# Hybrid attention/S5/MoE step on one core: a planner with VectorE's queue in its model, S5 units split, and output products that begin with the S5 rows

## The chip, the cores and the metric

The kernel runs on one core of a Trainium2 chip. The metric is device microseconds (us) of one execution. The kernel before took 1464.19 us (median of 3 runs, 1458.98 to 1472.08).

## The reference, cut to what matters

One layer, for a prompt of 1024 tokens (no cache) and for 8 decode sequences with one token each and 8192 cached positions in pages of 128. D = 1024, all data float32.

```python
hn = rmsnorm(x, ln1_g)
proj = hn @ w_in                      # columns: q 512 | k 512 | v 512 | u 512
q, k = rope_partial(q, pos) * 64**-0.5, rope_partial(k, pos)
# differential attention, 4 heads, two score maps a head (c = 0, 1)
s = einsum('bqhcd,bkhcd->bhcqk', q, k);  p = softmax(where(mask, s, -1e30))
a = p[:, :, 0] - lam * p[:, :, 1]
attn = subln(einsum('bhqk,bkhe->bqhe', a, v)) * (1 - lambda_init)
# S5: 32 groups of 16 channels, a 64-dim complex diagonal state each
a_cum, h = associative_scan(combine, (lam_bar, b_bar @ u));  h = h + a_cum * h0
y = gelu(real(c @ h) + d_skip * u);  s5_out = y * sigmoid(y @ w_glu + b_glu)
x = x + concatenate([attn, s5_out], -1) @ w_out      # rows 0:512 attention, 512:1024 S5
# top-1 of 4 groups, top-2 of 8 experts in it, 32 gated-MLP experts
x = x + hier_moe(rmsnorm(x, ln2_g), ...)
y = rmsnorm(x, ln_f_g)                # also returned: new k, v, last S5 states
```

## The kernel before, in words

Everything ahead of the experts is one long stage in which three kinds of work share the engines. The work is cut into *units*; `make_plan` (line 181) puts them in one order, `PLAN`, and TensorE, VectorE and GpSimd each walk through that same order and do their part of each unit; ScalarE walks through `ACT_PLAN`, the same units sorted by a modelled time (lines 262 and 263). Nothing is reordered at run time: an engine that waits for a semaphore in one unit holds back all later units on that engine.

`streams` (line 81) holds the lists, each unit with its TensorE cost and what must have ended how many us before it. `make_plan` is greedy: of the list heads that are ready it takes the one whose list stands first (`dec, C, O, T, S, qt, fin, s5, proj, q, late`), otherwise the one that is ready soonest. Only TensorE's time is kept; the time of the other engines stands in the lags. The lists are:

- `dec`: the decode attention. 64 units `K` (two passes over 4 sequences) and 64 units `V`, each with 8 pages of 256 KB of the cache, which SyncE loads into `ring` (16 slots) with line 500 as TensorE frees them. Between them `m1`, `m2`, `m3`, `pt` (row maximum, exp, transposes), and at the end `ov`, `dout`, `dout2`, `out(8)` (the decode rows' output product), `hT(8)`, `r(8)`. In the plan two K/V units stand at least `PACE` = 7.1 us apart.
- `proj` and `q`: products of the input projection in halves of 4 k-tiles (8 matmul records each), `kt`/`qt` transposes after VectorE's rotation.
- `S`, `C`, `T`, `O` for each of 8 query tiles i and 4 heads h: scores (TensorE), row maximum (VectorE, lines 1139 to 1145), exp (ScalarE, line 828), combination of the two maps (`C`, VectorE, lines 1152 to 1157), transposes (`T`, line 1919), copy (ScalarE, line 837), product with V (`O`); after the fourth head a root on GpSimd (line 563) and `AN` (line 1180), `ot` (line 1937).
- `s5`: `s5a` (tables, VectorE) and four rounds n of `bU` (GpSimd loads U in small pieces, line 618), `bA`, `bP`, `bK` (a product; VectorE adds `dd` at line 1381; GpSimd spreads the result with 8 loads, line 633), `bE`, `bX(n, 0..3)`, `bH` (VectorE: 12 passes over 512 columns with 8 scans between them, and small ones for the last states, lines 1396 to 1428), `bY(n, 0..1)`, `bG`, `bS`; `ld1` brings the result back for `glu`.
- `late`: `ld2` (first half of `w_out`, after the last `q`), `glu`, `ld3` (after the last `O`: second half of `w_out` at line 663, then the 8 tiles of x and the decode rows at lines 668 and 669), then for each of 8 row tiles i `out(i, a, f)`: column half a, k half f, 4 matmuls of 512 columns. A product keeps its PSUM bank from f = 0 to f = 1. `out` on TensorE (line 2099) waits for both halves of `w_out` and for all attention tiles; VectorE's addition to x (line 1463) waits for all x tiles.
- `fin`: `hn`, `hs`, `hT`, `r` for each tile (norm, transposes, router product), then the routing: `pick1`, `pick2`, `rank`, `rt0`, `rt1`, `ids`, `lists`, `turn0`.

`psum_keys` gives each unit its PSUM banks: six banks are handed out in a ring in plan order, and `hold` (line 174) is the planner's guess how long after the unit's end a bank stays taken. In `make_plan` the decode pages have a model of their own:

```python
land.append(max(land[-1], t + PAGE_LAG) + PAGE_US)     # 3.6, 6.0
due = max(due + PACE, t - 2 * PACE)                    # 7.1
```

In SBUF the first half of `w_out` lies where `w_q` was, the second where the attention's probabilities `P` are; x tiles 0 to 3 lie over `kT`, 4 to 7 over `V`. After that stage an expert loop runs over 4 experts at a time (3 MB of weights each), its first product waiting for the router of the decode rows; then the results are gathered and normed.

Of the kernel before, what the change touches and what calls it, by code (L numbers as in the profile page):

```python
# [18 lines left out]
SPP = 4  # L19
# [60 lines left out]

def streams():

    dec = [(("dprep",), 2.5, [(("dq",), 6.0)])]
    for x in range(NPASS):
        for t in range(TURNS):
            for g in range(2):
                for y in range(SPP):
                    dec.append((("K", x, t, g, y), 1.95, [(("ov", SPP * x - 1), 0.8)] if x else [(("dprep",), 0.5)]))
        dec += [(("m1", x), 0.8, [(dec[-1][0], 0.9)]), (("m2", x), 0.3, [(("m1", x), 3.3)]),
                (("m3", x), 0.3, [(("m2", x), 1.0)]), (("pt", x), 2.3, [(("m3", x), 3.2)])]  # L90
        for y in range(SPP):
            b = SPP * x + y
            for t in range(TURNS):
                for g in range(2):
                    late = [(("pt", x), 1.2)] if t + g + y == 0 else [(("ov", b - 2), 1.2)] if t + g == 0 and y >= 2 else []
                    dec.append((("V", x, y, t, g), 1.95, late))
                    if y and t == 0 and g == 1:
                        dec.append((("ov", b - 1), 0.5, [(("V", x, y - 1, TURNS - 1, 1), 2.5)]))
        dec.append((("ov", b), 0.5, [(("V", x, y, TURNS - 1, 1), 2.5)]))
    dec += [(("dout",), 0.1, [(("ov", NB - 1), 1.0)]), (("dout2",), 0.2, [(("dout",), 2.0)]),  # L100
            (("out", NT), 4.0, [(("dout2",), 1.0), (("out", NT - 1, 1, 1), 0.0)]), (("hn", NT), 0.0, [(("out", NT), 2.0)]),
            (("hs", NT), 0.0, [(("hn", NT), 2.5)]), (("hT", NT), 1.0, [(("hs", NT), 0.8)]),
            (("r", NT), 1.1, [(("hT", NT), 0.6), (("r", NT - 1), 0.0)])]
# [22 lines left out]
    qt = [(("qt", i), 0.6, [(("q", i, 1), 3.5)] + ([(("S", i - 1, H - 1), 0)] if i else [])) for i in range(NT)]  # L126
# [3 lines left out]
    for n, (i, h) in enumerate(heads):  # L130
        w = 0.128 * (i + 1)
        x = [(("qt", i), 1.5)] + ([(("O",) + heads[n - 2], 0)] if n >= 2 else [])
        S.append((("S", i, h), 0.28 + 0.22 * (i + 1), x))
        C.append((("C", i, h), 0.0, [(("S", i, h), 3.3 + 3.0 * w)]))
        T.append((("T", i, h), 0.14 * (i + 1), [(("C", i, h), 0.9 + 1.1 * w)]))
        x = [(("T", i, h), 0.5 + 0.8 * w)]
        if h == 0 and i:
            x.append((("ot", i - 1), 0))
        O.append((("O", i, h), 0.2 + 0.37 * (i + 1), x))
        if h == H - 1:  # L140
            O += [(("AN", i), 0.0, [(("O", i, h), 3.0)]), (("ot", i), 0.66, [(("AN", i), 0.8)])]

    s5 = [(("s5a",), 0.0, [(("dprep",), 2.0)])]
    for n in range(NQ):
        x = [(("bY", n - 1, 1), 0)] if n else [(("u", 3, 1, 1), 4.0), (("dk2",), 3.0), (("s5a",), 60.0)]
        s5 += [(("bU", n), 0.0, x + [(("u", n, 1, 1), 3.0)]), (("bA", n), 0.0, x), (("bP", n), 1.1, [(("bA", n), 5.0)]),
               (("bK", n), 2.1, [(("bA", n), 11.0)]), (("bE", n), 0.0, [(("bK", n), 2.5)])]
        s5 += [(("bX", n, j), 0.75, [(("bP", n), 2.2), (("bU", n), 14.0)]) for j in range(JQ)]
        s5 += [(("bH", n), 0.0, [(("bX", n, JQ - 1), 1.2)])]
        s5 += [(("bY", n, 0), 3.5, [(("bH", n), 13.5), (("bK", n), 13.0)]), (("bG", n, 0), 0.0, [(("bY", n, 0), 2.0)]),  # L150
               (("bY", n, 1), 3.5, []), (("bG", n, 1), 0.0, [(("bY", n, 1), 2.0)]),
               (("bS", n), 0.0, [(("bG", n, 1), 1.5)])]
# [2196 lines left out]
```

## Time and profile before

| | us |
|---|---|
| median of 3 runs | 1464.19 (1458.98 to 1472.08) |
| the profiled execution, own time | 1464.86 |
| its span | 1463.1, mean granted clock 0.94 |
| busy: TensorE / weight loads / VectorE / ScalarE / GpSimd | 1279.2 / 670.6 / 521.6 / 248.5 / 214.7 |
| DMA | 458.31 MB, mean 313 GB/s |
| K and V pages | 1024 transfers of 256 KB, 4.7 us each to land |

Times in the profile count from the span's start. A line is that of the helper for most matmuls (line 1800), so matmuls are told apart by tile and by their place in time; one float32 matmul leaves two records, a transpose one. The granted clock is TensorE's, 1.00 being the level of 2.4 GHz and 0.50 that of 1.2 GHz.

### The profile page before, as it was taken

What the parts mean: (1) busy time and instruction counts of PE and PEld (TensorE: products, weight loads), DVE (VectorE), ACT (ScalarE), POOL (GpSimd) and SP (SyncE); (2) the same over time, 40 slices, a digit from 0 to 9 for tenths busy, and PEclk for the clock granted to TensorE, in tenths of its full rate; (3) what the DMA queues carried; (4) which work ended last, traced back from release to release, by engine and by line L of the source; (5) the groups of instructions that cost most, each with busy time, mean ns of one, the idle gap of its engine ahead of it and who ended that gap; (6) DMA issues with size and microseconds to landing.
All of it is one profiled execution on the core that took longest, in us unless ns stands there. A gap on an engine that the chain in (4) does not pass through costs nothing.

```text
span 1463.1 us, 26568 instructions
## 1 busy us (share of the span) xinstructions
PE 1279.2 (87%) x9000; PEld 670.6 (46%) x9000; DVE 521.6 (36%) x1413; ACT 248.5 (17%) x476; POOL 214.7 (15%) x329
## 2 busy tenths in 40 slices
PE   7999999999869799998869999976899999999930
PEld 4545555554324346666544444433444444444410
DVE  2723543253365455553512111153122111121126
ACT  2101111121212233332212000000011111111111
POOL 2003140313100200000010000001122222222211
PEclk9999999999989999998999999976999999999975
DMA  9989998869968999999996998998899999999764
GB/s 364 329 310 293 321 294 283 272 198 298 298 227 304 352 338 363 365 315 323 331 387 228 330 336 293 322 349 321 277 324 371 360 354 363 361 363 366 256 211 179
DMA packets 185201, 458.31 MB, mean 313 GB/s; under 512 B 23953, under 2 KB 24337, under 8 KB 176530
## 3 DMA queue, kind: packets, MB, share of 16 engines
q1 hardware_dynamic: 163602, 390.21, 75.4%
q0 software_dynamic: 21504, 66.78, 13.8%
q8 instruction: 66, 1.08, 0.3%
q14 instruction: 29, 0.24, 0.0%
HBM read 421.92 MB, written 33.80 MB: 311 GB/s over the span
## 4 chain that ended last, share of the span: by engine, by line
PE 70%; DMA 12%; DVE 7%; SPq 5%; issue 3%; DVEq 2%; ACT 1%; POOL 0%; ACTq 0%; POOLq 0%
PE WA L1800 52%; PE SC L1800 7%; PE OD L1800 7%; DMA ring<-in_cacheK 6%; SPq L500 4%; DMA qpad<-h_scratch,idc 3%; DMA ring<-in_cacheV 2%; PE WA L2166 2%; DVE arena L1769 1%; PE WA L1919 1%; DVE arena L1782 1%; DVE st L1141 1%; PE WA L2126 1%; DMA arena<-y_scratch 1%; DVEq L1771 1%
## 5 line engine op out<-in xcount | busy, mean ns | idle before, releaser
L1800 PE MATMUL WA<-arena 128*128 128x512 f32 (+10 forms) x1440 | 353.4, 432 | 17.6 <-issue 7.2
L1800 PE MATMUL WA<-arena,xm 128*128 128x512 f32 (+3 forms) x816 | 313.6, 581 | 8.4 <-DMA arena<-in_w_out 6.5
L1800 PEld LDWEIGHTS WA<-arena 128*128 128x128 f32 (+2 forms) x1440 | 191.6, 195 | 155.0 <-issue 135.5
L1800 PEld LDWEIGHTS WA<-arena,xm 128*128 128x128 f32 (+1 forms) x816 | 124.4, 174 | 162.8 <-issue 154.7
L1800 PE MATMUL WA<-xm,arena 128*128 128x512 f32 x192 | 87.3, 603 | 1.7 <-ACT arena L958 1.3
L1800 PE MATMUL OD<-ring,sall 128*32 128x512 f32 x512 | 71.0, 670 | 15.0 <-DMA ring<-in_cacheV 15.0
L563 POOL TENSOR_TENSOR st<-st,consts 128x1 f32<-128x1 f32 (+2 forms) x18 | 13.8, 765 | 466.2 <-DVEq L1175 280.0
L1800 PE MATMUL OD<-ring,qpad 128*32 128x128 f32 x2048 | 67.9, 285 | 15.7 <-DMA ring<-in_cacheK 15.7
L1800 PEld LDWEIGHTS OD<-ring,qpad 128*32 128x32 f32 x2048 | 56.6, 114 | 35.9 <-DMA ring<-in_cacheK 18.4
L1800 PE MATMUL SC<-ring,qpad 128*32 128x128 f32 x2048 | 64.9, 278 | 9.1 <-DMA ring<-in_cacheK 9.0
L1712 DVE TENSOR_TENSOR xm<-WA,colw 128x960 f32<-128x960 f32 x16 | 18.5, 1158 | 147.2 <-PE WA L2166 147.2
L1712 DVE TENSOR_TENSOR arena<-WA,colw 128x960 f32<-128x960 f32 x16 | 18.5, 1158 | 139.5 <-PE WA L2166 139.3
L1800 PEld LDWEIGHTS SC<-ring,qpad 128*32 128x32 f32 x2048 | 55.0, 111 | 24.5 <-issue 12.0
L1800 PE MATMUL SC<-ring,sall 128*32 128x512 f32 x512 | 61.4, 598 | 2.2 <-DMA ring<-in_cacheV 2.2
L828 ACT ACTIVATE arena<-WA,st 128x128 f32<-128x128 f32 (+7 forms) x64 | 47.4, 740 | 80.0 <-DVEq L1145 77.9
L686 POOL DMA_DIRECT2D y_dec<-arena x32 | 17.8, 556 | 271.7 <-ACT arena L965 271.7
L1800 PE MATMUL WA<-ring,xm 128*128 128x512 f32 x128 | 56.3, 592 | 0.0
L1800 PE MATMUL WA<-xm 128*128 128x512 f32 x128 | 56.3, 592 | 0.0
L965 ACT ACTIVATE arena<-WA 128x1024 f32<-128x1024 f32 x32 | 32.7, 1023 | 128.7 <-PE WA L1800 128.7
L1800 PEld LDWEIGHTS WA<-xm,arena 128*128 128x128 f32 x192 | 35.4, 192 | 41.6 <-issue 40.1
L1463 DVE TENSOR_TENSOR arena<-arena,WA 128x512 f32<-128x512 f32 x16 | 11.0, 688 | 113.9 <-PE WA L1800 113.9
L1141 DVE TENSOR_REDUCE st<-WA 128x1 f32<-128x128 f32 (+7 forms) x64 | 48.5, 758 | 5.1 <-issue 0.4
(364 smaller groups left out, 1244.1 us busy)
## 6 DMA issues: line engine op xcount, KB each, us to landing
ring<-in_cacheK SPq DMA_DIRECT2D x512, 256.0 KB, 4.7
ring<-in_cacheV SPq DMA_DIRECT2D x512, 256.0 KB, 4.7
arena<-in_w_gu SPq DMA_DIRECT2D x16, 2048.0 KB, 9.8
arena<-in_w_dn SPq DMA_DIRECT2D x16, 1024.0 KB, 14.3
ring<-in_w_gu SPq DMA_DIRECT2D x8, 2048.0 KB, 10.3
xm<-in_w_gu SPq DMA_DIRECT2D x8, 2048.0 KB, 10.5
ring<-in_w_dn SPq DMA_DIRECT2D x8, 1024.0 KB, 14.8
xm<-in_w_dn SPq DMA_DIRECT2D x8, 1024.0 KB, 14.8
```

The source lines that it names most:

```text
L500: sp.dma_start(ring[:, GRP * half + j, :], cache[bass.ds(pages[j], 1), :, :] .rearrange("a p n -> p (a n)")).then_inc(s_pg[PARTS * half + ...
L686: gp.dma_start(io["y_dec"][bass.ds(4 * NB * q + NB * v, NB), :], yb[v % 2][CAP:128, :]).then_inc(m_sd[v % 2], 16)
L828: act.activation(P[:, n % 2, c, 0:w], slot("S", i, h, c)[:, 0:w], ACT.Exp, bias=st[:, 4 * (n % 2) + c:4 * (n % 2) + c + 1], scale=HD ** -0 ...
L965: act.activation(yb[v % 2], W[1][:, :], ACT.Copy).then_inc(m_ys, 1)
L1141: dve.reduce_max(st[:, 8 + c:9 + c], S[:, 0:w], AX)
L1712: dve.tensor_tensor(hgT[v % 2][:, :, 0:CAP], (W[0] if src is None else src)[:, :] .rearrange("p (k n) -> p k n", k=KD)[:, :, 0:CAP], colw[ ...
L1769: dve.scalar_tensor_tensor(x1[0:r, i, :], yg[i][c][0:r, :], wts[0:r, c, i:i + 1], x1[0:r, i, :], MUL, ADD)
L1771: dve.drain()
L1782: dve.scalar_tensor_tensor(x1[0:r, i, :], x1[0:r, i, :], st[0:r, i:i + 1], lnf[0:r, :], MUL, MUL)\
L1800: return pe.matmul(out, lhsT, rhs, start=first, stop=last, **kw)
L1919: last = pe.transpose(slot("AT", i, h)[:, 128 * j:128 * j + 128], P[:, n % 2, 0, 128 * j:128 * j + 128], ident)
L2166: last = pe.transpose((W[0] if out is None else out)[:, 128 * k:128 * k + CAP], hg[v % 2][0:CAP, 128 * k:128 * k + 128], ident[0:CAP, 0:CAP])
```

## The change

The planner gets VectorE's time. `vector_us(unit)` gives for each unit the us that VectorE needs and the lag from TensorE's end to its start; `make_plan` keeps `busy`, the end of VectorE's queue in plan order, and records `end[("dve",) + unit]`. Dependencies that stood on lags after TensorE's end now stand on VectorE's end, and banks are counted free from there. TensorE costs of T, O, bY, bX, bK, rank, ids and others are changed too.

```diff
+def vector_us(unit):
+    ...
+    if k in ("u", "k", "q", "out") and (len(a) == 1 or a[-1] == 1):
+        return {"u": (1.1, 0.2), "k": (1.25, 0.95), "q": (1.25, 0.95), "out": (0.75, 0.2)}[k]
+    return {
+        "S": (1.95 + 0.265 * i, 0.2), "C": (0.95 + 0.133 * i, 0.0), "O": (1.35 if a[1:] == (H - 1,) else 1.15, 0.2),
+        "AN": (0.7, 0.0), "s5a": ((4.0, 9.0, 9.0, 9.0)[i if k == "s5a" else 0], 3.0 if a == (1,) else 0.0),
+        "bA": ((4.0, 5.0)[a[1] if k == "bA" else 0], 0.0), "bE": (3.9, 0.0), "bK": (0.3, 1.3),
+        "bH": ((3.7, 3.0, 5.6)[a[1] if k == "bH" else 0], 0.0), "bY": (0.75, 0.9), "bG": (0.75, 0.8),
+        ...
+    }.get(k)
...
-        w = 0.128 * (i + 1)
-        x = [(("qt", i), 1.5)] + ([(("O",) + heads[n - 2], 0)] if n >= 2 else [])
+        w = 0.115 * (i + 1)
+        x = [(("qt", i), 1.0)] + ([(("O",) + heads[n - 2], 0)] if n >= 2 else [])
         S.append((("S", i, h), 0.28 + 0.22 * (i + 1), x))
-        C.append((("C", i, h), 0.0, [(("S", i, h), 3.3 + 3.0 * w)]))
-        T.append((("T", i, h), 0.14 * (i + 1), [(("C", i, h), 0.9 + 1.1 * w)]))
-        x = [(("T", i, h), 0.5 + 0.8 * w)]
+        C.append((("C", i, h), 0.0, [(dve("S", i, h), 0.9 + w)]))
+        T.append((("T", i, h), 0.12 * (i + 1), [(dve("C", i, h), 0.25)]))
+        x = [(("T", i, h), 0.5 + w)]
...
-        O.append((("O", i, h), 0.2 + 0.37 * (i + 1), x))
+        O.append((("O", i, h), 0.2 + 0.21 * (i + 1), x))
...
+    late += [(("ldx",), 0.0, [(("S", NT - 1, H - 1), 0.1)])]
+    o7 = [(("ld3",), 0.0, [(("O", NT - 1, H - 1), 0.1)])]
...
-        x = [(("ld3",), 9.0), (("glu", 4, 0), 2.5), (("ot", NT - 1), 1.0)]
-        late += [(("out", i, a, f), half, x) for a in range(2) for f in range(2)]
+        x = [(("ldx",), 7.0), (("ld2",), 16.0), (dve("glu", 4, 0), 0.2)], [(("ld3",), 8.0), (("ot", i), 1.6)]
+        late += [(("out", i, a, f), half, x[f]) for f in range(2) for a in range(2)]
...
-        end[unit] = t
+        end[unit] = done = t
+        if vector_us(unit):
+            us, lag = vector_us(unit)
+            end[("dve",) + unit] = done = busy = max(busy, t + lag) + us
...
-                free[b] = t + hold(unit)
+                free[b] = done + hold(unit)
```

S5 units are split: `s5a` into four parts (a generator that yields), `bA` into two (before and after `s_pA`), `bH` into three: the products before the scans, the scans, the rest. Their instructions are the same, in the same order among themselves; other units can stand between the parts. GpSimd's stores of `bH` belong to the last part.

```diff
-            def bH(n):
+            def bH(n, p):
...
+                if p == 0:
+                    dve.wait_ge(s_Xs, JQ * (n + 1))
...
+                    return
+                if p == 1:
+                    for j in range(JQ):
...
+                    return
```

The output products take the S5 rows (k tiles 4 to 7) first, and `w_out`'s halves are loaded in that order; each half has a semaphore of its own. x tiles 0 to 3 are loaded after the last `S`, the others with `ld3`. In the plan both column halves do f = 0, then both f = 1.

```diff
             def ld2():
                 gp.wait_ge(*filled("q", NT - 1))
-                gp.dma_start(wout[:, 0:4, :], io["w_out"][:, 0:4, :]).then_inc(s_wo, 16)
+                gp.dma_start(wout[:, 0:4, :], io["w_out"][:, 4:8, :]).then_inc(s_wo, 16)
+
+            def ldx():
+                gp.wait_ge(*filled("S", NT - 1, H - 1, 1))
+                for i in range(4):
+                    gp.dma_start(x1[:, i, :], io["x_p"][i, :, :]).then_inc(s_x1, 16)
 
             def ld3():
                 gp.wait_ge(*filled("O", NT - 1, H - 1))
-                gp.dma_start(wout[:, 4:8, :], io["w_out"][:, 4:8, :]).then_inc(s_wo, 16)
+                gp.dma_start(wout[:, 4:8, :], io["w_out"][:, 0:4, :]).then_inc(s_wo2, 16)
...
-                for i in range(NT):
+                for i in range(4, NT):
...
             def out_(i, a=0, f=0):
                 if f == 0:
-                    pe.wait_ge(s_wo, 32)
-                    pe.wait_ge(s_mix, NT)
+                    pe.wait_ge(s_wo, 16)
                     pe.wait_ge(s_mix2, 9)
+                else:
+                    pe.wait_ge(s_wo2, 16)
+                    pe.wait_ge(s_mix, i + 1)
```

## Rows read from the trace of the kernel before

**Rows 1.** Windows, stages: length, busy PE PEld DVE ACT POOL, PEclk, DMA share, GB/s
```profile
377.00:748.00 371.00, 319.99 (x3322) 186.19 (x3323) 196.79 (x542) 105.29 (x232) 25.44 (x40) 0.94 0.92 324
748.00:951.00 203.00, 193.29 (x998) 85.71 (x997) 32.46 (x60) 14.57 (x28) 11.69 (x22) 0.97 0.88 312
951.00:1025.00 74.00, 51.97 (x334) 26.04 (x327) 34.70 (x114) 2.53 (x5) 5.44 (x7) 0.72 0.92 335
1025.00:1463.00 438.00, 367.49 (x1088) 176.33 (x1085) 104.52 (x225) 64.58 (x115) 87.31 (x105) 0.93 0.88 315
```
**Rows 2.** Timeline of TensorE: the first K unit, the routing's ids product, the last V units
```profile
43.70 3.70 PE L1800 MATMUL SC<-ring,qpad 128*32 128x128 f32 x128
...
993.46 7.07 PE L1800 MATMUL WA<-arena 128*128 128x52 f32 x32 [4.11 <-DVEq L1669]
1000.46 5.11 PE L1800 MATMUL OD<-ring,sall 128*32 128x512 f32 x32
```
**Rows 3.** Waits of TensorE, 30 to 1025 us: total, times, longest
```profile
PE OD L1800 <- DMA ring<-in_cacheK: 15.7, 7, 4.2
PE OD L1800 <- DMA ring<-in_cacheV: 15.0, 8, 5.8
PE WA L1919 <- DVEq L1159: 14.3, 3, 11.1
PE SC L1800 <- DMA ring<-in_cacheK: 9.0, 6, 2.5
PE WA L1937 <- DVEq L1181: 7.6, 4, 3.4
...
PE WA L1800 <- DMA arena<-in_w_out: 6.5, 1, 6.5
```
**Rows 4.** Windows inside the attention stage and at the pass's turn
```profile
390.00:440.00 50.00, 35.70 (x174) 14.21 (x172) 31.34 (x106) 8.75 (x27) 2.49 (x3) 0.83 0.64 226
440.00:750.00 310.00, 274.08 (x3130) 168.23 (x3132) 159.64 (x419) 94.00 (x197) 20.75 (x33) 0.96 0.96 339
780.00:790.00 10.00, 10.00 (x39) 5.36 (x38) 1.17 (x4) 6.15 (x11) 0.00 (x0) 1.00 0.01 3
```
**Rows 5.** Timeline of TensorE, 417 to 436 us: T(1,0) and q(3,0)
```profile
429.05 0.69 PE L1919 MATMUL WA<-consts,arena 128*128 128x128 f32 x2 [11.13 <-DVEq L1159]
429.53 5.55 PE L1800 MATMUL WA<-arena,xm 128*128 128x512 f32 x8
```
**Rows 6.** Timeline of VectorE, 414 to 429 us: first and last of bH(3), then C(1,0)
```profile
414.17 0.69 DVE L1396 TENSOR_TENSOR arena<-arena 128x512 f32<-128x512 f32 x1
...
420.98 0.69 DVE L1410 TENSOR_TENSOR arena<-arena 128x512 f32<-128x512 f32 x1
...
426.10 0.29 DVE L1428 TENSOR_TENSOR rt<-rt,arena 128x32 f32<-128x32 f32 x2
...
428.47 0.49 DVE L1157 SCALAR_TENSOR_TENSOR arena<-arena,st 128x256 f32<-128x256 f32 x1
```
**Rows 7.** Timeline of TensorE: the first output products, and a K unit between them
```profile
756.93 5.77 PE L1800 MATMUL WA<-arena,xm 128*128 128x512 f32 x8 [6.48 <-DMA arena<-in_w_out]
...
766.33 1.08 PE L1800 MATMUL OD<-ring,qpad 128*32 128x128 f32 x32 [2.62 <-DMA ring<-in_cacheK]
767.59 5.37 PE L1800 MATMUL WA<-arena,xm 128*128 128x512 f32 x8 [0.18 <-PE OD L1800]
...
773.99 3.70 PE L1800 MATMUL WA<-arena,xm 128*128 128x512 f32 x8
```
**Rows 8.** GpSimd's last issues before the output products: w_out's second half, x
```profile
746.42 0.59 POOL L663 DMA_DIRECT2D arena<-in_w_out  x1
747.01 4.16 POOL L668 DMA_DIRECT2D arena<-in_x_p  x8
```
**Rows 9.** VectorE's waits before line 1381 (bK of the four S5 rounds)
```profile
  ACT arena L894: 27.4, 2
  DMA arena<-in_ddiag: 17.3, 2
```

More of the change, by code:

```diff
@@ L125, in streams @@
         qs += [(("q", i, 0), half, x), (("q", i, 1), half, [])]
[L126 removed]
+    qt = [(("qt", i), 0.5, [(dve("q", i, 1), 0.3)] + ([(("S", i - 1, H - 1), 0)] if i else [])) for i in range(NT)]
     S, C, T, O = [], [], [], []
@@ L144, in streams @@
+    s5 = [(("s5a", 0), 0.0, [(dve("dprep"), 0.0)])] + [(("s5a", p), 0.0, [(dve("s5a", p - 1), 1.3)]) for p in range(1, 4)]
     for n in range(NQ):
[L145 to L148, printed above, removed]
@@ new lines, in streams @@
+        late += [(("out", i, a, f), half, x[f]) for f in range(2) for a in range(2)]
+        fin += [(("hn", i), 0.0, [(dve("out", i, 1, 1), 0.1)]), (("hs", i), 0.0, [(dve("hn", i), 0.9)]),
+                (("hT", i), 0.95, [(dve("hs", i), 0.25)]), (("r", i), 0.6, [(dve("hT", i), 0.25)])]
+    fin += [(("pick1",), 0.0, [(dve("r", NT - 1), 0.1)]), (("pick2",), 0.0, [(dve("pick1"), 0.0)]),
+            (("rank",), 4.7, [(dve("pick2"), -1.5)]), (("rt0",), 0.0, [(("rank",), 0.3)]), (("rt1",), 0.0, [(dve("rt0"), 0.0)]),
+            (("ids",), 6.9, [(dve("rt1"), 0.3)]), (("lists",), 0.0, [(("ids",), 0.3)]),
+            (("turn0",), 1.0, [(("lists",), 14.0), (("out", NT), 0.0)])]
@@ L171, in streams @@
+    return {"dec": dec, "o7": o7, "C": C, "O": O, "T": T, "S": S, "qt": qt, "fin": fin, "s5": s5, "proj": proj, "q": qs,
             "late": late}
 def hold(unit):
-    k, w = unit[0], 0.128 * (unit[1] + 1) if len(unit) > 1 else 0
-    return {"S": 3.0 + 3.0 * w, "T": 0.5 + 0.8 * w, "O": 0.5, "pt": 1.3, "bY": 5.0, "bP": 1.5, "bK": 1.6,
-            "bX": 0.8, "q": 0.8, "k": 0.8, "v": 0.8, "hT": 1.5, "out": 1.0}.get(k, 1.0)
+    k, w = unit[0], 0.115 * (unit[1] + 1) if len(unit) > 1 else 0
+    return {"S": 0.7 + w, "T": 0.5 + w, "O": -0.5, "pt": 1.3, "bP": 1.5, "bK": 1.0, "out": 0.1, "u": 0.1, "hT": 0.1, "r": 0.1,
+            "bX": 0.8, "q": -0.4, "k": -0.4, "v": 0.9, "ot": 1.4, "glu": -0.8, "ids": 4.0, "rank": 16.0}.get(k, 1.0)
@@ L187, in make_plan @@
     land, gone, due = [4.0, 10.0], [], 4.0
-    kept, never = {}, 1e9
+    kept, never, busy = {}, 1e9, 0.0
     def place(unit):
@@ L226, in make_plan @@
         for b in kept.get(unit, []):
-            free[b] = t + 1.0
+            free[b] = done + hold(unit)
         if unit[0] in "KV":
@@ L259, in hymba_step @@
     SPOT, USES = banks(PLAN)
-    ready = {u: ends.get(u, ends.get(u[:-1], 0.0)) + (2.4 if u[0] == "S" else 0.0) for u in PLAN}
+    ready = {u: ends[("dve",) + u] - (0.9 + 0.13 * u[1]) if u[0] == "S" else ends.get(u, ends.get(u[:-1], 0.0)) for u in PLAN}
     ACT_PLAN = sorted(PLAN, key=lambda u: ready[u])
@@ L1264, in cmul, with s5a_parts @@
                 dve.drain()
-            def s5a():
+            def s5a_parts():
                 dve.wait_ge(s_ld5, 32)
```

145 lines of the change are left out of this document (83 added, 62 removed), and 3 rows, old and new, of the table i.

## The prediction

> **What bounds the kernel now.** I read the busy times of the windows first, to find the stages [rows 1]. The change can act only on what lies ahead of the experts, the first 1025 us; the 438 us behind are an expert loop whose code stays as it is, and I carry them over. Before 1025 us two resources are nearly full. TensorE is busy 320.0 of 371 us in the attention stage (377 to 748 us) and 193.3 of 203 us around the output products (748 to 951 us); the DMA engines have shares of 0.92 and 0.88 there. Neither is the bound alone, so what counts is where each of them stands still.
>
> Next the list of who waited for whom on TensorE [rows 3]. Its largest rows are waits for K and V pages: 15.7 + 15.0 + 9.0 = 39.7 us. Waits on VectorE come second: 14.3 us before T units and 7.6 us before `ot`. Then 6.5 us once for `w_out`. Only the second and third kind are what the change speaks of.
>
> The decode stream is the other end of the stage. Its first K unit starts at 43.7 us and its last V unit ends at 1000.46 + 5.11 = 1005.6 us [rows 2]: 961.9 us for 128 units, 7.5 us each. The planner puts them 7.1 us apart, in both kernels, so 128 x 7.1 = 909 us is the least that this plan allows, and 961.9 - 909 = 53 us is the most that any rearrangement within the pace can bring. So the ceiling is 53 us, before any stall is named.
>
> **The change part by part.** The sum is made against the profiled execution's own 1464.9 us (span 1463.1 us), which is 0.7 us above the median of the runs; that difference is far below what can be measured, and I forecast both alike.
>
> *A. bH in three parts, VectorE in the plan.* TensorE stood 11.1 us before T(1,0), and the q half behind it ran at 1.2 GHz for a part: 5.55 us [rows 5] in place of 3.70 us for the same 8 records [rows 7], 1.85 us more. The reason is in VectorE's timeline [rows 6]: from 414.17 to 426.4 us it works on bH(3) without a gap, and C(1,0), for which T(1,0) waits, is done only at 428.96 us. Split, the attention's units can stand between the parts, whose longest is the third, 420.98 to 426.4 us, 5.4 us. DMA was not full here: share 0.64 in 390 to 440 us [rows 4], so the ring had nowhere to load, and what TensorE gains the stream gains too. Bounds: 0 (the next plan has the same collision elsewhere) to -13.0 us (11.1 + 1.85). I take -11: near the full row, less 2 us for a part that is still in the way.
>
> *B. The small VectorE waits of the attention stage.* T has 14.3 - 11.1 = 3.2 us left, `ot` 7.6 us: 10.8 us [rows 3]. But from 440 to 750 us the DMA share is 0.96 [rows 4], so only 0.04 x 310 = 12 us of the stream's time is free there, and TensorE's K units are met by missing pages anyway. Most of this gain turns into a longer wait for K. Bounds: -10.8 to +6 us (a new order can place as many new waits as half of the old ones); I take -3.
>
> *C. Output products begin with the S5 rows.* Before, the first half product starts at 756.93 us after 6.5 us of waiting for `w_out`, takes 5.77 us, the next 5.37 us, and one at the full clock 3.70 us [rows 7]: 6.5 + 2.1 + 1.7 = 10.2 us lost. Now the S5 rows' half of `w_out` is there (loaded after the last q), and out(0,0,0) and out(0,1,0) can run as soon as the last scores are made, so 2 x 3.6 = 7.2 us of work fill the hole, and the halves behind it come after work rather than after a gap. More than two halves cannot go: in the list the third needs the attention rows, which are issued at 746.42 us [rows 8] as before, since their place is held by P. VectorE's wait for all x tiles goes too, but it had banks to spare and I cost it at nothing; the cover is the 5 other banks. The stage behind is TensorE's (193.3 of 203 us), so what is saved goes through, up to the stream: its share of 0.88 there [rows 1] leaves 0.12 x 203 = 24 us. Bounds: 0 to -14 us (both numbers above, partly overlapping); I take -8.
>
> *D. The tail.* The routing holds TensorE 4.1 us before `ids`, and the last 2 V units stand behind its 7.07 us [rows 2], pages landed or not. The plan's new costs for rank, ids and the routing on VectorE may put V ahead. Bounds: -5 to +4 us, the wait itself in either direction; I take -2.
>
> *E. x tiles 0 to 3 ahead of the last K units.* 2 MB now start with the last scores, some 15 us before the 746.42 us of before, in a stretch whose DMA share is 0.96 [rows 4]. At 339 GB/s of that row they take 6.2 us, which the K units there wait, and which ld3 has less behind. The net is a wait moved from beside the output products into the attention chain. Bounds: 0 to +6 us; I take +3. The Trainium skill (DMA: Bandwidth & Descriptors, Issuing engines are not separate DMA queues) says that transfers issued by GpSimd and by SyncE run on the same 16 engines and interleave; by it an earlier start on GpSimd's queue frees nothing as long as the pages fill the engines. The trace agrees with the direction: a K unit waits 2.62 us while `w_out` and x are in flight [rows 7].
>
> *F. Instructions.* s5a, bA and bH issue what they did; two semaphores and one wait are new, nothing that an engine would show. The S5 loads and their 8 small pieces a round stay, and so does most of the 39.7 us for pages.
>
> Sum: -11 - 3 - 8 - 2 + 3 = -21 us, so 1464.9 - 21 = **1444 us**. All lower ends give -13 - 10.8 - 14 - 5 = -43 us, 1422; all upper ends +6 + 4 + 6 = +16 us, 1481.
>
> **The rivals.**
>
> *Rival 1: the page stream takes it all back, 1460 us.* For it: the pace of 7.1 us is unchanged, 0.96 of DMA in the second half of the attention, and pages are already TensorE's largest wait. Then A's gain is spent waiting for pages by 750 us, C's work fills time in which K is late anyway, and only some 5 us remain, 1464.9 - 5 = 1460. Against it: the share of 0.64 over 50 us, and 0.01 over the 10 us from 780 [rows 4]: there is DMA time to recover.
>
> *Rival 2, the slower side: VectorE stands in S5's loads with the attention behind it, 1480 us.* Before line 1381 (bK) VectorE waited 27.4 + 17.3 = 44.7 us over the four rounds, for GpSimd's U loads and for a product [rows 9]. These were free, since TensorE had projection halves that need nothing of VectorE. The new plan counts VectorE's busy time but nothing of how late a load is in traffic: bK has 1.3 us and 0.3 us in its table. If it packs rounds 2 and 3 against scores and combinations, each such wait holds up the S and C units queued behind it on VectorE, then T and O on TensorE and `out`. It decides the sign from the point where 21 of the 44.7 us, 47%, are exposed; at 80% the price is 36 us, 1444 + 36 = 1480. Against it: three of the four rounds lie before the attention, where no unit of TensorE hangs on VectorE closely. The Trainium skill (Perfetto Trace Analysis, Tensor Engine Instruction (MATMUL, LD_WEIGHTS)) says that VectorE's execution FIFO is strict, unlike TensorE's; by this more places to stand in, now nine parts where there were three units, speak against the split. Rows 6 show such a queue: C(1,0) came behind all of bH(3).
>
> *Rival 3: VectorE's and `w_out`'s waits all go and the stream follows, 1427 us.* 11.1 + 1.85 + 10.8 + 10.2 + 4.1 = 38 us, 1464.9 - 38 = 1427, within the ceiling of 53. It needs a greedy order that is right nearly everywhere, and pages that come earlier in a stretch with 0.96.
>
> **How the numbers follow.** About 1% (14.6 us) is what a measurement of this kernel can tell from no change; the bound for faster is 1449.6 us. The forecast's case, 1432 to 1455 us, has 0.55, of which 0.44 lies below 1449.6. Rival 1 has 0.22, rival 2 0.13, rival 3 0.10. Faster: 0.44 + 0.10 = 0.54; within 1%: 0.11 + 0.22 = 0.33; slower: 0.13. The predicted time is the likeliest case's, 1444. The range for 8 in 10 takes in that case, rival 1 and a part of either outer case, 1425 to 1470: below, 1422 and 1427 bound it; above, half of rival 2's price, 1444 + 18 = 1462, and some of the +16 us sum.
>
> **What would show it.** Right: no wait over 4 us of a T unit on line 1159, and DMA share over 0.8 in the 50 us around the fourth bH; two output halves before the last `ot`, and both f = 1 halves at 3.7 us; the last V ends near 985 us instead of 1005.6 and the experts start near 1004. For rival 1: waits for pages above 50 us in the same list and a last V later than 997 us. For rival 2: VectorE's wait before line 1381 or 1396 ending in the attention stage, with T or `ot` waiting just then. For E: K waits over 3 us between 725 and 745 us beside x loads. I would be wrong altogether if the new plan moves S5's fourth round so late that `glu`, and with it the S5 rows, is not ready when the scores end.

## The result: 1% slower, and the profile after

| | before | after |
|---|---|---|
| median of the runs | 1463.0 us | 1479.1 us (1478.3 to 1481.8) |
| ratio after to before | | 1.0118 [1.0077, 1.0158] |
| span of the profiled execution | 1463.1 us | 1477.4 us |
| the 128th V unit, V(1,3,3,1), ends | 1005.6 us | 1018.9 us |
| last router product r(8) ends | 1025.5 us | 1040.0 us |

The forecast was 1444 us with a range of 1425 to 1470; the change costs 16 us and lies outside. The ratios, here and below, leave out runs in a slower state that now and then befalls any kernel, and they differ from the ratios of the medians by up to 0.3%. Behind r(8) the two traces have 437.6 and 437.4 us, so all of the 14.3 us between the spans comes from the part ahead of the experts.

The same stages as [rows 1], after the change, then the 50 us of the fourth bH [rows 4] and two stretches at the turn of the pass (columns as in [rows 1]):

```profile
377.00:748.00 371.00, 341.15 (x3257) 198.03 (x3256) 189.36 (x532) 105.01 (x229) 21.93 (x34) 0.94 0.91 320
748.00:951.00 203.00, 190.71 (x1063) 88.45 (x1061) 38.46 (x76) 15.76 (x30) 13.30 (x23) 0.98 0.84 292
951.00:1025.00 74.00, 52.90 (x240) 19.00 (x240) 25.56 (x91) 0.24 (x1) 1.39 (x2) 0.59 0.95 348
390.00:440.00 50.00, 47.24 (x253) 21.33 (x246) 22.22 (x80) 9.35 (x26) 11.18 (x21) 1.00 0.97 344
725.00:775.00 50.00, 38.81 (x483) 25.27 (x483) 12.32 (x28) 8.20 (x16) 6.37 (x11) 0.90 1.02 379
775.00:805.00 30.00, 28.35 (x148) 14.96 (x150) 8.28 (x18) 7.34 (x13) 1.63 (x3) 1.00 0.25 92
```

The hole at 390 to 440 us is closed: TensorE busy 47.2 us in place of 35.7, DMA share 0.97 in place of 0.64. And in 775 to 805 us the DMA engines stand: share 0.25. TensorE's waits, 30 to 1025 us, as [rows 3]:

```profile
PE OD L1861 <- DMA ring<-in_cacheK: 20.0, 9, 4.1
PE OD L1861 <- DMA ring<-in_cacheV: 15.0, 13, 5.0
PE WA L1980 <- DVEq L1199: 13.9, 7, 3.4
PE SC L1861 <- DMA ring<-in_cacheV: 13.9, 8, 3.8
PE SC L1861 <- DMA ring<-in_cacheK: 4.2, 3, 2.2
PE WA L1861 <- DVEq L1730: 2.8, 1, 2.8
PE WA L1861 <- DMA arena<-in_w_out: 2.5, 1, 2.5
```

The single wait of 11.1 us before a T unit (now line 1980) is gone, its longest is 3.4 us, but there are seven that add up to 13.9 us where three made 14.3. Pages: 53.1 us where [rows 3] with its smaller rows has 41.9.

**Where the 14 us arise.** I laid each unit of the planner's order onto TensorE's records. Three lengths add up to the end: the end of the last K unit, the turn of the pass from there to the end of V(1,0,0,0), and the V phase from there to r(8).

| us | last K unit | turn | V phase | r(8) |
|---|---|---|---|---|
| before | 767.4 | 25.1 | 233.0 | 1025.5 |
| after | 773.3 | 31.4 | 235.3 | 1040.0 |

So 5.9 us in front of the last K unit, 6.3 us in the turn, 2.3 us behind. Meanwhile the last output product ends 10.8 us earlier (940.0 for 950.8) and `ids` 7.3 us earlier, for nothing: TensorE then waits for V pages, 5.0 us once and 0.8 us before each of the last five groups.

**The turn.** TensorE's timeline after the change. pt(1) is line 2048; in it ScalarE's exponentials of the whole pass are transposed, so nothing of V(1) can start before it:

```profile
777.27 1.18 PE L1861 MATMUL OD<-knT,qpad 128*32 128x8 f32 x32
778.38 3.70 PE L1861 MATMUL WA<-arena,xm 128*128 128x512 f32 x8
782.03 3.60 PE L1861 MATMUL WA<-arena,xm 128*128 128x512 f32 x8
785.56 0.38 PE L1861 MATMUL OD<-consts,rt 1*128 1x1 f32 x2
785.87 3.70 PE L1861 MATMUL WA<-arena,xm 128*128 128x512 f32 x8
789.40 1.04 PE L2190 MATMUL WA<-consts,arena 128*128 128x128 f32 x8
790.28 3.60 PE L1861 MATMUL WA<-arena,xm 128*128 128x512 f32 x8
793.71 1.87 PE L1861 MATMUL WA<-wr,arena 128*128 128x36 f32 x16
795.41 3.68 PE L1861 MATMUL WA<-arena,xm 128*128 128x512 f32 x8
798.93 0.60 PE L2048 MATMUL WA<-consts,sall 128*128 128x128 f32 x4
```

ScalarE's side, where the exponentials end at 788.5 us and the copies of pt (line 905) follow 11 us later:

```profile
786.20 2.00 ACT L896 ACTIVATE sall<-sall,mrow 128x2048 f32<-128x2048 f32 x1 [6.75 <-DVEq L1248]
788.20 0.28 ACT L898 ACTIVATE snew<-snew,mrow 128x8 f32<-128x8 f32 x1
799.57 2.69 ACT L905 ACTIVATE sall<-WA 128x512 f32<-128x512 f32 x4 [10.99 <-PE WA L2048]
```

Between 788.5 and 798.9 us TensorE runs the end of an output half, hT(0), a half, r(0) and another half. It isn't waiting; the planner put them there, because pt takes five of the six PSUM banks at once. The change makes a tile's f = 0 halves first, for both column halves, and then the f = 1 halves, so two banks are held by unfinished sums at a time and a third is just being opened: in its plan pt(1) stands behind out(1,1,1), r(0) and out(2,0,0). pt(1) comes only 10.4 us after its input. In the kernel before, out(1,0,0) had just ended and pt(1) began at 785.0 us, 0.4 us behind the exponentials. During the extra time the ring is full and no page is loaded, which is the share of 0.25.

### The profile page after: what moved, and what is told of

Its sections match the earlier page's. It is cut to its first block, busy times and chain, and to the rows that moved or that the text cites. A ratio compares the mean times of both kernels' runs of the same rounds, so it can differ in the third digit from the quotient of the medians.

```text
span 1477.4 us, 26567 instructions
## 1 busy us (share of the span) xinstructions
PE 1301.8 (88%) x9000; PEld 681.8 (46%) x9000; DVE 521.8 (35%) x1413; ACT 248.3 (17%) x476; POOL 214.9 (15%) x329
## 4 chain that ended last, share of the span: by engine, by line
PE 71%; DMA 11%; SPq 7%; DVE 6%; issue 3%; DVEq 1%; ACT 0%; POOL 0%; ACTq 0%; POOLq 0%
PE WA L1861 53%; PE SC L1861 7%; PE OD L1861 6%; SPq L530 6%; DMA ring<-in_cacheK 5%; DMA ring<-in_cacheV 3%; PE WA L2230 2%; PE WA L1980 1%; DVE st L1181 1%; DMA ring<-h_scratch,idc 1%; DVE arena L1830 1%; DVE arena L1843 1%; SPq L524 1%; DMA arena<-y_scratch 1%; DVEq L1832 1%
## 5 line engine op out<-in xcount | busy, mean ns | idle before, releaser
L1861 PE MATMUL OD<-ring,sall 128*32 128x512 f32 x512 | 75.4, 702 | 15.0 <-DMA ring<-in_cacheV 15.0
L593 POOL TENSOR_TENSOR st<-st,consts 128x1 f32<-128x1 f32 (+2 forms) x18 | 13.9, 775 | 493.2 <-DVEq L1215 286.0
L1861 PE MATMUL SC<-ring,sall 128*32 128x512 f32 x512 | 67.2, 641 | 15.5 <-DMA ring<-in_cacheV 13.9
L1861 PE MATMUL SC<-ring,qpad 128*32 128x128 f32 x2048 | 68.2, 289 | 4.2 <-DMA ring<-in_cacheK 4.2
L1861 PEld LDWEIGHTS SC<-ring,qpad 128*32 128x32 f32 x2048 | 58.2, 116 | 19.7 <-issue 12.0
L972 ACT ACTIVATE arena<-arena 128x1024 f32<-128x1024 f32 (+1 forms) x9 | 9.5, 1056 | 214.6 <-DVEq L1533 214.1
```

Source lines behind the costliest of these rows:

```text
L1861: return pe.matmul(out, lhsT, rhs, start=first, stop=last, **kw)
```

## The experiments

Sixteen kernels beside the two. The medians of the kernel before beside them were 1462.6 (first four), 1461.9, 1462.9 and 1465.9 us. What was measured stands in one table per group, with each profiled execution's three lengths. That execution is one of the runs and can lie off their median: af_p680's is its slowest (1484.6 us), oo_af_xl_lag12's lies 7 us above, and the others are within 5 us.

### One part alone, and one bank less

`plan_only`: the change's planner and split S5 units with the output part of the kernel before. `out_only`: the planner before with the change's output part. `wait_pt` and `order_af`: the changed kernel with one line of the list altered.

```diff
 wait_pt
+        x = (x[0] + ([(("pt", 1), 0.0)] if i else []), x[1])
 order_af
-        late += [(("out", i, a, f), half, x[f]) for f in range(2) for a in range(2)]
+        late += [(("out", i, a, f), half, x[f]) for a in range(2) for f in range(2)]
```

> Only the planner with VectorE's time and the split S5 units; loads of w_out and x, the waits of the output products and their order in the list are those of the kernel before. Theory 1 (the turn of the decode pass): the loss comes from the output part, which puts the five-bank unit pt(1) 10.4 us behind its exp and the last K page 5.9 us later, while the V phase behind it has a fixed length (213.1 us before, 214.2 us after). It expects pt(1) within 2 us of the end of exp and 1455 to 1465 us, at or under the kernel before. Theory 2 (the front): the planner part is at fault, by S5 rounds that stand ahead of the v and q products and collide with page loads; it expects 1475 us or more.

> Only the output part: S5 rows first, halves of w_out in that order, x tiles in two groups, both column halves with f = 0 before f = 1; the planner's costs and the S5 units are those of the kernel before. Theory 1: pt(1) stands 10 us or more behind the end of its exp, V(1,0,0,0) starts 10 to 15 us later than before and the time is 1473 to 1480 us. Theory 2: the output part is neutral or a gain, 1450 to 1464 us.

> The changed kernel with one dependency more in the planner: the first halves (f = 0) of the output products of tiles 1 to 7 stand behind pt(1) in the list. Theory 1: pt(1) follows its exp within 2 us, V(1,0,0,0) starts 8 to 11 us earlier than in the changed kernel and the time falls by as much, to 1468 to 1471 us, although the output products end some 12 us later. Theory 2: 1479 us or more, since output work is held back.

> The changed kernel with the old order inside a tile (each column half does f = 0 and f = 1 before the next), so that one PSUM bank less is held open; all else as changed. Theory 1: the planner finds pt(1) its banks 8 us sooner, V starts 6 to 9 us earlier, 1470 to 1473 us. Theory 2: no change from 1479 us beyond 3 us.

| | median | ratio to before | last K | turn | V phase |
|---|---|---|---|---|---|
| plan_only | 1480.2 | 1.0137 [1.0096, 1.0178] | 778.4 | 27.0 | 235.8 |
| out_only | 1478.1 | 1.0128 [1.0088, 1.0169] | 761.9 | 37.0 | 235.1 |
| wait_pt | 1468.9 | 1.0048 [1.0024, 1.0072] | 769.0 | 27.0 | 231.9 |
| order_af | 1464.3 | 1.0027 [0.9991, 1.0062] | 769.0 | 23.5 | 231.9 |

The bank theory holds: either line that lets pt(1) come when its input is there gives back 10 to 15 us, order_af more than the 6 to 9 us I had expected of it. In order_af:

```profile
777.66 3.60 PE L1861 MATMUL WA<-arena,xm 128*128 128x512 f32 x8
781.19 0.38 PE L1861 MATMUL OD<-consts,rt 1*128 1x1 f32 x2
781.50 3.70 PE L1861 MATMUL WA<-arena,xm 128*128 128x512 f32 x8
785.03 0.60 PE L2048 MATMUL WA<-consts,sall 128*128 128x128 f32 x4
```

order_af's r(8) is 15.6 us earlier than the changed kernel's: 7.9 are the turn and 3.4 the V phase; 4.3 stand in front of the last K unit. The two orders are equal up to the last O, and that O ends at 743.9 us there and at 748.9 us in the changed kernel, so these 4.3 are scatter between executions and not the banks' doing. out_only has the longest turn of all, and loses in spite of the earliest last K of the four. But plan_only missed: I expected 1455 to 1465, and the planner alone loses 17.6 us too, with a turn that is only 2 us longer. The two halves of the change lose 17.6 and 15.5 us each, and together 16: they do not add.

### Why the planner alone loses, and what a stop in attention costs

`plan_lag14`: in plan_only the planner takes `w_out`'s second half to arrive 14 us after the last O, not 9. `delay`: order_af with 26 reductions on VectorE ahead of C(1,0). `af_p680`: order_af with a pace of 6.8 us. `xlate2_lag17`: order_af with `w_out` taken 17 us late and x tiles 2 to 8 sent late.

```diff
 plan_lag14
-        x = [(("ld3",), 9.0), ...
+        x = [(("ld3",), 14.0), ...
 delay
+                if (i, h) == (1, 0):
+                    for z in range(26):
+                        dve.reduce_sum(dumb[:, z:z + 1], P[:, n % 2, 1, 0:256], AX)
 af_p680
-PAGE_US, PAGE_LAG, PACE = 6.0, 3.6, 7.1
+PAGE_US, PAGE_LAG, PACE = 6.0, 3.6, 6.8
 xlate2_lag17 (and the lag of w_out 17.0 for 8.0)
-                for i in range(4, NT):
+                gp.wait_ge(s_score, 4 * TURNS)
+                for i in range(2, NT):
                     gp.dma_start(x1[:, i, :], io["x_p"][i, :, :]).then_inc(s_x2, 16)
```

> The planner and the split S5 units alone, with the kernel before's output part, and one number changed in the planner: the second half of w_out is taken to arrive 14 us after the last O, not 9 (in the trace of the run with the planner alone it came 11 to 17 us after). The plan then has the K units (1,3,1,2) ahead of the first output product, as in the kernel before. Theory 1 (the loss of the planner alone is a place in TensorE's order: out(0,0,0) waits 5.4 us for w_out with two K units behind it, so ring slots come free late and the last K unit ends 11 us later): the last K unit ends at 763 to 769 in place of 778.4, pt(1) 20 us behind it, the time 1461 to 1468, that is 12 to 18 us below the run without it. Theory 2 (the loss comes from the first 700 us, VectorE's or the pages', whatever the order there): 1476 to 1481.

> The changed kernel with each column half's two products one behind the other (1464.3 us), and 26 reductions of 128x256 put on VectorE ahead of C(1,0), some 11 us by the rate of the rows for such reductions (26 x 0.42): the wait that the change took out of the attention stage, put back at the same place. Theory 1 (attention's waits are covered: the page stream is late by its own transfers and takes the gain): +0 to +4, 1464 to 1468, the page waits behind it smaller by about as much as the wait put in. Theory 2 (a stop of TensorE in attention comes out at the end at full length, and the gain was lost elsewhere): +9 to +12, 1473 to 1476.

> The changed kernel with each column half's two products one behind the other, both last K units ahead of every product that needs the second half of w_out (arrival taken as 17 us), x tiles 0 and 1 as in the change, and the seven others (3.1 MB) sent only when TensorE has finished the last K unit, into the time in which the page stream stands for the turn of the pass (DMA share 0.25 to 0.46 in 775 to 800). Theory 1 (the end is the last K unit's end, plus the turn, plus the V phase of 231 to 236 us): the last K unit at 758 to 763 in place of 769.0, V(1,0,0,0) 22 to 25 us later, the end at 1455 to 1460. Rival (the moved transfers only move the wait: the V pages or the additions of x are late in their place): 1463 to 1470.

> The changed kernel with each column half's two products one behind the other, and the planner's pace of the page units 6.8 us in place of 7.1. In the plan the last K unit comes 15 us earlier and the last V unit 4 us. Theory 1 (the stream runs at what the DMA gives, share 0.93 in nearly every stretch, and the plan's places only decide what waits): within 4 us of 1464.3, with page waits up by 5 us or more. Theory 2 (the planner's pace holds the stream back): 1455 to 1460.

| | median | ratio to before | last K | turn | V phase |
|---|---|---|---|---|---|
| plan_lag14 | 1473.6 | 1.0066 [1.0033, 1.0100] | 772.1 | 25.1 | 236.1 |
| delay | 1479.6 | 1.0147 [1.0077, 1.0217] | 780.8 | 23.7 | 231.9 |
| xlate2_lag17 | 1464.3 | 1.0026 [0.9990, 1.0063] | 765.3 | 23.5 | 236.8 |
| af_p680 | 1476.2 | 1.0095 [1.0066, 1.0123] | 763.9 | 32.8 | 247.7 |

`delay` settles the largest question of the prediction. The reductions took 8.6 us, and TensorE stood where the kernel before had stood:

```profile
464.60 8.59 DVE L1195 TENSOR_REDUCE dumb<-arena 128x1 f32<-128x256 f32 x26 [0.17 <-issue]
```

```profile
463.99 0.70 PE L1865 MATMUL WA<-arena 64*128 64x256 f32 x4
474.25 0.69 PE L1984 MATMUL WA<-consts,arena 128*128 128x128 f32 x2 [9.56 <-DVEq L1203]
```

The end came 15.3 us later in the medians, 12.1 us in the profiled spans, and 11.8 us of these stand already at the last K unit. My theory 1, that the page stream swallows such a stop, is false; a stop of TensorE in the attention comes out at the end at full length. Whether it costs more than its length isn't shown: the intervals of the two ratios leave anything from 6 to 29 us. The ring holds 16 pages and is full soon after TensorE stops; then DMA stops too. The kernel before shows it beside its 11 us wait (windows of before):

```profile
417.00:432.00 15.00, 3.87 (x11) 1.89 (x11) 13.19 (x43) 0.65 (x2) 2.49 (x3) 0.59 0.46 159
432.00:437.00 5.00, 5.00 (x23) 1.61 (x22) 2.23 (x8) 0.86 (x4) 0.00 (x0) 0.86 0.00 0
```

So the gain of the removed wait was real, and something else in front takes it away. af_p680, for which both my theories had 1468 us at most, says it isn't the pace: the last K unit came earlier, as in its plan, but attention ran late (the last O at 769.3 us, not 743.9) and the run lost 12 us. plan_lag14 gives 6.6 us back by the position of one product in TensorE's order, less than expected: it still had one K unit 9.0 us behind pages. xlate2_lag17 missed: last K came 3.7 us earlier, and the V phase grew by 4.9. Since it differs from order_af in two things, it can't tell what late x tiles are worth; the last group does.

### The split of bH on the old planner

`split_h`: the kernel before with bH in three units and nothing else in the code. I had expected TensorE's order to stay the same; it does so only from V(0,0,2,0) on. Ahead of that, in the projection, the parts' lags move bY, bP, bK and some K units and halves by a place or a few, so the run measures the split together with these moves. `oo_af_lag12`: the kernel before with the output part, in order_af's order, `w_out` taken 12 us late. `split_oo`: both. `split_oo_xl`: both, and x tiles 2 to 8 sent when TensorE has finished the last K unit.

```diff
 split_h
-        s5 += [(("bH", n), 0.0, [(("bX", n, JQ - 1), 1.2)])]
+        s5 += [(("bH", n, 0), 0.0, [(("bX", n, JQ - 1), 1.2)])]
+        s5 += [(("bH", n, p), 0.0, [(("bH", n, p - 1), 4.5)]) for p in range(1, 3)]
```

> The kernel before with one thing of the change: bH is three units on VectorE, 4.5 us apart in the list, and everything else is as it was; TensorE's order stays the same, and VectorE has 3.7 us of bH(3) ahead of C(1,0) in place of 12.3. Theory 1 (a stop of TensorE in attention comes out at the end at full length and more, as in the run with 11 us of reductions, and the planner's own order gives the gain away again by more short stops, each with a slow clock behind it): the wait at T(1,0) is 2 to 4 us in place of 11.1, the slow clock behind it shorter, and the time 1450 to 1455 against 1462. Theory 2 (the change's gain is lost because the stream takes it, whatever the planner): 1459 to 1463.

> The kernel before with the output part alone, each column half's two products one behind the other, and the second half of w_out taken to arrive 12 us after the last O, so that both last K units stand ahead of every product that needs it. Theory 1 (end = last K unit + turn + V phase; with two halves one behind the other no third bank is held, and the turn is that of before, 24 to 26 us, not 37 as in the run with the output part alone): last K unit at 760 to 766, V(1,0,0,0) at 785 to 791, time 1455 to 1461. Theory 2 (rows of S5 first cost the stream something of their own, as x tiles ahead of pages): 1465 or more.

> Both of the runs before in one: the kernel before, bH in three units, and the output part with each column half's products one behind the other and w_out taken to arrive 12 us after the last O. If the two parts add, as theory 1 has it (a stop less in attention, the same turn): 1443 to 1452. If the stream bounds both: no better than the better of the two, 1455 to 1460.

> The run before, with the seven x tiles from 2 on sent only when TensorE has finished the last K unit, tiles 0 and 1 as in the change. Theory 1 (x tiles ahead of the last K pages are the 2 to 6 us by which that unit is late): 2 to 5 below the run before it. Rival (with the kernel's own order of K units, pages are no longer behind x tiles, or the V phase is as much longer, as the run with the planner of the change and late x tiles had it, 0.0 against its base): within 1.5 of the run before it.

| | median | ratio to before | last K | turn | V phase |
|---|---|---|---|---|---|
| split_h | 1455.8 | 0.9934 [0.9903, 0.9965] | 766.3 | 24.4 | 228.3 |
| oo_af_lag12 | 1471.7 | 1.0062 [1.0026, 1.0099] | 774.6 | 25.5 | 232.9 |
| split_oo | 1460.9 | 0.9965 [0.9928, 1.0001] | 765.4 | 24.9 | 232.3 |
| split_oo_xl | 1452.2 | 0.9894 [0.9854, 0.9934] | 757.4 | 24.4 | 231.3 |

split_h is the change's one good part (1455.8 us; I expected 1450 to 1455): T(1,0) waits 3.2 us and the q half behind it takes 4.8 us instead of 5.55.

```profile
420.83 0.69 PE L1926 MATMUL WA<-consts,arena 128*128 128x128 f32 x2 [3.18 <-DVEq L1162]
421.31 4.80 PE L1807 MATMUL WA<-arena,xm 128*128 128x512 f32 x8
```

oo_af_lag12 missed by 10 us. Its last K unit waited for pages, twice, behind `w_out` and the x tiles on the same DMA engines:

```profile
764.77 1.94 PE L1810 MATMUL OD<-ring,qpad 128*32 128x128 f32 x32 [7.41 <-DMA ring<-in_cacheK]
772.67 1.94 PE L1810 MATMUL OD<-ring,qpad 128*32 128x128 f32 x32 [5.96 <-DMA ring<-in_cacheK]
```

and taking 3.1 MB of x out of that stretch (split_oo_xl) moved the last K unit by 8.0 us and the median by 8.7. split_oo missed as well: had its two parts added as I expected, it would have come to 1443 to 1452 us, and it took 1460.9.

### Late x tiles by themselves

Four kernels differ from one above only in that x tiles 2 to 8 are sent when TensorE has finished the last K unit (the edit of xlate2_lag17).

> The run with the change's planner alone and w_out taken 14 us late (1473.6), with x tiles 2 to 8 sent only when TensorE has finished the last K unit. Theory 1 (that planner brings the last O forward against the page stream, so that w_out and 4.5 MB of x go ahead of four K units' pages and not three; 3.1 MB less at 400 GB/s are 8 us): the last K unit at 763 to 766 in place of 772.1 and the time 1463 to 1468. Rival (the loss is in the slow clock and in waits in front and in the V phase, not here): 1470 or more.

> The changed kernel itself, with x tiles 2 to 8 sent only when TensorE has finished the last K unit; the order of the products and the place of pt(1) are left as the change has them. Theory 1: the last K unit 4 to 7 us earlier than 773.3, the turn still 30 to 32 us since pt(1) still stands behind out(1,1,1), the time 1471 to 1475. Rival (a late x tile holds a bank longer and the turn grows by what the pages gain): 1477 or more.

> The kernel before with bH in three units and x tiles 2 to 8 sent only when TensorE has finished the last K unit; its own order of output products. If the S5 rows first are worth nothing of their own: 1449 to 1454, as the run that has them (1452.2). If they are worth several us: 1455 or more.

> The run with the output part alone, halves one behind the other, w_out taken 12 us late (1471.7), with x tiles 2 to 8 late. Theory 1 (x ahead of pages was its loss: K pages waited 16.7 us in one slot behind them): the last K unit at 762 to 767 in place of 774.6, the time 1459 to 1464, that is 7 to 9 above the run that has bH split too. Rival: 1467 or more.

| late x tiles in | without | with | ratio to before | last K | turn | V phase |
|---|---|---|---|---|---|---|
| plan_lag14 | 1473.6 | 1466.1 | 1.0019 [0.9985, 1.0053] | 774.6 | 23.4 | 233.4 |
| the changed kernel | 1479.1 | 1472.6 | 1.0064 [1.0025, 1.0102] | 763.5 | 31.4 | 237.3 |
| split_h | 1455.8 | 1448.0 | 0.9905 [0.9869, 0.9941] | 750.9 | 23.3 | 230.9 |
| oo_af_lag12 | 1471.7 | 1461.2 | 0.9962 [0.9924, 0.9999] | 768.5 | 25.3 | 232.7 |

With split_oo_xl that makes five pairs, and all gain, by 6.5 to 10.4 us, near the 3.1 MB at some 400 GB/s, 8 us. Four of the pairs have their two runs in different groups; by the ratios to the kernel before beside each, the gains are 4 to 15 us. Taken alone only the pairs of oo_af_lag12 and split_oo are clear of the intervals; it is the five together that show it. In plan_lag14_xl the profiled execution was 7.7 us late already at K(1,2,1,3), so its last K shows nothing; from that unit to the last K it is 62.4 us where plan_lag14 has 67.6. The changed kernel keeps its turn of 31.4 us, as expected. Between 735 and 800 us TensorE waits 7.2 us for `w_out` and 4.8 us for K pages in split_h, 6.7 and 0.5 us with late x tiles. Windows of split_h, and then of split_h_xl, first about from the last O to the last K unit and then to V(1,0,0,0), columns as before:

```profile
741.00:767.00 26.00, 13.52 (x209) 8.55 (x209) 1.79 (x5) 1.52 (x5) 6.23 (x11) 0.83 1.02 397
767.00:791.00 24.00, 24.00 (x118) 11.35 (x120) 6.70 (x15) 6.19 (x11) 0.75 (x2) 0.97 0.42 156
```

```profile
725.00:752.00 27.00, 16.94 (x251) 11.12 (x240) 1.79 (x5) 2.55 (x6) 3.42 (x6) 0.87 1.03 386
752.00:775.00 23.00, 23.00 (x121) 11.02 (x123) 6.71 (x15) 6.19 (x11) 3.99 (x8) 1.00 0.62 234
```

The first stretch is full either way; the bytes went into the turn, whose DMA share rises from 0.42 to 0.62 without lengthening it. **split_h_xl, at 1448.0 us, is faster than both kernels**, by 1% and 2%. It has the old order of output products. With the S5 rows first the same kernel is split_oo_xl, by the medians 4.2 us slower (by the ratios 1.6 us faster, so the two can't be told apart), and split_oo is 5.1 us slower than split_h, also within the intervals: the output part in its best form shows no gain here.

## Why the prediction was wrong

*Step C, the output products, is the step that failed.* Its mechanism came as told: out(0,0,0) at 741.5 us and out(0,1,0) at 748.8 us, both before the last `ot`, and the last output product 10.8 us earlier (I took 8); only the first f = 1 half still took 6.38 us at 762.23, not 3.7. What failed is "the stage behind is TensorE's, so what is saved goes through, up to the stream". The stage ends with a V unit, V waits for the turn, and products that come earlier shorten neither. The sum had no term for the banks at the turn. Where I spoke of them, I put them at nothing, since there are "5 other banks"; pt(1) needs five of the six, in a stage in which the change holds one more open. Undoing it gave 10.2 us back by wait_pt and 14.8 by order_af; in the profiles 4.4 and 7.9 of these are the turn and 3.3 and 3.4 the V phase. I had read the share of 0.01 in 780 to 790 us [rows 4] as DMA time to recover by the pages; it is the sign of a ring that is full behind a turn, and lengthening the turn lengthens it. Other transfers can use it, as the late x tiles do. out_only has steps C and E alone: -8 + 3 = -5 us in my sum, +15.5 measured.

*Step A was right in mechanism and by itself two thirds of its size; what else the new plan does was not in the sum.* The wait went, the share around the fourth bH rose to 0.97, above the 0.8 I had named. By itself, on the old planner, the split is worth 7.1 us and not 11 (the moved units of the projection included): 3.2 us of wait stay, and the slow clock with them. In the changed kernel not even this arrives: plan_only has steps A, B and D, -16 us in my sum, and measured +17.6. The sum had no term for what the new order would do to TensorE's clock and to its place among the pages; 6.6 us of the 17.6 are one product ahead of a K unit (plan_lag14). At K(1,2,1,3) both kernels have done the same units, save one `ot`, at 710.2 and 710.1 us. TensorE's waits from 30 to 715 us fell from 65.6 to 53.9 us, and its busy time rose by 11.3 us for the same work:

```profile
30.00:715.00 685.00, 619.36 (x6012) 351.32 (x6015) 328.00 (x971) 148.79 (x305) 104.66 (x184) 0.96 0.90 306
```

```profile
30.00:715.00 685.00, 630.65 (x5976) 357.85 (x5975) 327.86 (x970) 146.09 (x300) 104.75 (x184) 0.95 0.90 305
```

(the first of before, the second of after). The granted clock is what differs. Its time at 1.2 GHz between 30 and 715 us adds up to 54.6 us before and 73.6 us after, in 10 pieces before and 11 after, most of them right behind a stop. TensorE was busy for 40.9 us of it before and for 66.3 after; at half speed that is 20.4 and 33.2 us of work lost, and the difference, 12.7 us, covers the 11.3. It isn't the number of stops: before there are 10 of 2 us and more (39.0 us together), after 9 (28.2 us). Before, the longest slow piece (13.7 us) lies for 9 us inside the wait of 11.1 us, where it costs nothing. After, the slow pieces fall on work, for instance behind a V page that comes 3.8 us late:

```profile
368.77 1.93 PE L1861 MATMUL SC<-ring,sall 128*32 128x512 f32 x8 [3.79 <-DMA ring<-in_cacheV]
```

```profile
362.00:372.00 10.00, 4.91 (x30) 0.89 (x26) 1.85 (x3) 0.93 (x3) 2.62 (x6) 0.82 1.06 316
372.00:382.00 10.00, 10.00 (x23) 4.46 (x23) 7.34 (x16) 1.08 (x2) 0.58 (x1) 0.67 0.74 273
```

The ten kernels of this case with the change's planner have a mean granted clock of 0.921 to 0.938 in all their runs, the kernel before 0.931 to 0.949. Every trace bears the reading out. Up to K(1,2,1,3), TensorE is busy at 1.2 GHz for 37 to 41 us in the four kernels with the old planner and bH whole, for 42 to 57 in the four with bH split on it, for 51 to 66 in nine with the change's planner and for 75 in af_p680; with half of it taken off, the busy time is 594 to 597 us in all but the last. Which stops bring how much slow clock was not tested, and it scatters: the nine have one and the same order there. What was tested is the size: plan_lag14_xl against split_h_xl, which differ in the planner, the other split units and the order that comes of them, is 18 us. In their profiled executions 16.0 us of it (of 26.9) stand at K(1,2,1,3): 4.4 in waits, and 10.3 of the rest in clock.

*Step B* had the sign wrong within its bounds: T and `ot` waits went from 21.9 to 15.1 us, of which the 11.1 are A's, so the small ones grew by 4.3 us where I took -3.

*Step D* was right in the wait (`ids` 4.1 to 2.8 us) and idle in effect, since the last V units wait for pages there.

*Step E looked in the wrong place.* I took +3 from x tiles 0 to 3 alone; no run tests that move by itself, and its sign (K waits over 3 us between 725 and 745 us) did not come, with no such wait there and 5.2 us in all from 745 to 775 us, where before has 3.0. The five pairs say that x tiles ahead of the last K pages cost some 2.6 us per MB (8.2 us on average for 3.1 MB), and the last K unit of the changed kernel is 5.9 us late. That price stood already in the kernel before, where all 4.2 MB of x are issued from 747.01 us on [rows 8], ahead of the last K pages: split_h, which keeps this, gained 7.8 us by the medians. It was there to be won, and I looked only at what the change added. The Trainium skill's rule on issuing engines that I cited (DMA: Bandwidth & Descriptors, Issuing engines are not separate DMA queues), that transfers of all queues share the same 16 DMA engines, is borne out by all five pairs: with 3.1 MB taken from GpSimd's queue there, the way from K(1,2,1,3) to the last K unit became 2.0 to 10.4 us shorter, though SyncE's pages are as they were.

*The rivals.* Rival 1 had its signs (53.1 us of page waits, the last V at 1018.9 us, later than 997), but not its reason: `delay` shows that the stream doesn't absorb TensorE's stops. Rival 2 didn't occur. VectorE's wait before bK is still there,

```profile
L1434 DVE TENSOR_TENSOR arena<-arena 128x128 f32<-128x128 f32 x4 | 1.2, 292 | 42.7 <-ACT arena L934 24.1 <-DMA arena<-in_ddiag 18.7
```

42.7 us where [rows 9] has 44.7, but the fourth round now ends at 411.3 us (bY(3,1)), before the first S unit of attention ends at 413.5. The slower side came by a mechanism that I had not listed. Rival 3 fell with A and C.

## What to carry to other kernels

Where a stream must turn (a softmax between two passes), find the unit at the turn that needs the most of a shared resource, here five of six banks, and ask of every edit nearby what it holds open at that moment; then move transfers that nobody needs yet into the turn, where the DMA engines stand. An order that shortens waits on paper has to be judged by TensorE's busy time for the same work too: slow clock that fell into one long stop costs nothing there, and the same or more of it behind shorter stops falls on work. And a stage's busy share doesn't say who ends it: products finished 10 us earlier are worth nothing if a page ends the stage.

## What the runs showed of the hardware that I had not expected

TensorE's busy time at the full clock for the same work is the same within 4 us in 17 kernels (594 to 597 us up to K(1,2,1,3)), once half of its time at 1.2 GHz is taken off; what an order costs in clock can so be read from one trace. The kernel before, unchanged, had medians of 1461.9 to 1465.9 us beside the four groups but single runs from 1450 to 1479 us, and a run's time goes with its mean granted clock: in one group 0.949 at 1452.6 us, 0.943 at 1461.4, 0.934 at 1471.0. K(1,2,1,3) ends between 702.3 and 712.2 us in eight traces with the same order ahead of it. A profiled landmark of one execution is therefore good to some 5 us here, and only lengths between two landmarks carried the smaller findings.
